# Experts in column tiles: the second half of the blocks one slot behind the first

## What is computed

```python
scores = sigmoid(h @ router_w)                     # 1152 x 16
g      = best of 4 groups of 4 experts, by the sum of its two best scores
expert = the 2 best experts in that group; w = their scores, normed to sum 1
y[t]   = sum over the 2 experts e of t:  w * ((silu(h[t] @ gate[e]) * (h[t] @ up[e])) @ down[e])
```

## Time and profile before

| | |
|---|---|
| median of three runs | 2530.28 us (2527.90 to 2533.29) |
| the profiled execution | 2531.27 us, its span 2529.4 us |
| mean granted clock of TensorE | 0.98 of full speed |
| TensorE busy | 2356.9 us, 93% of the span |
| VectorE, ScalarE, GpSimd busy | 1282.3, 816.9, 897.9 us |
| first matmul of the expert loop, last step's down | 1914.01 us, 2471.05 us |
| loaded by SyncE's queue over the whole span | 280.57 MB |

### The profile page before, as it was taken

How to read it: one execution, slowest core, us unless ns; L and a number is a source line. 1 busy time by engine, 2 the same in 40 slices (tenths; PEclk the granted TensorE clock), 3 DMA queues, 4 the chain that set the end, 5 groups by cost and what they waited for, 6 DMA issues and landing times.

```text
span 2529.4 us, 42298 instructions
## 1 busy us (share of the span) xinstructions
PE 2356.9 (93%) x16564; PEld 1602.0 (63%) x16564; DVE 1282.3 (51%) x2061; ACT 816.9 (32%) x1598; POOL 897.9 (35%) x816
## 2 busy tenths in 40 slices
PE   5999999999999999999899999999987999889994
PEld 3555787777777777776677767775463444444453
DVE  5337565666336566785959926984361101101115
ACT  3132322232222233325277732221242222222224
POOL 0001343443666556765945445661000000000003
PEclk9999999999999999999999999999998999999998
DMA  8241111112212212421201234433037556856436
GB/s 333 75 159 67 46 55 51 53 55 88 90 51 73 67 46 81 172 78 36 87 29 38 93 143 163 129 118 126 1 143 280 197 196 255 322 231 269 147 135 233
DMA packets 83401, 316.83 MB, mean 125 GB/s; under 512 B 10428, under 2 KB 37636, under 8 KB 59396
## 3 DMA queue, kind: packets, MB, share of 16 engines
q1 hardware_dynamic: 71108, 280.57, 30.4%
q0 software_dynamic: 8928, 22.03, 2.5%
q10 hardware_dynamic: 3168, 11.54, 1.1%
HBM read 711.76 MB, written 63.71 MB: 307 GB/s over the span
## 4 chain that ended last, share of the span: by engine, by line
PE 73%; DMA 9%; DVE 8%; ACT 5%; issue 3%; POOL 2%; SPq 1%; DVEq 0%; ACTq 0%; POOLq 0%
PE psum L835 24%; PE psum L723 9%; PE psum L1800 9%; PE psum L611 8%; DMA arena<-in_moe 7%; PE psum L1658 5%; PE psum L1784 4%; PE psum L1385 2%; ACT arena L2130 1%; PE psum L635 1%; PE psum L1273 1%; PE psum L1247 1%; PE psum L1769 1%; PE psum L1600 1%; PE psum L1373 1%
## 5 line engine op out<-in xcount | busy, mean ns | idle before, releaser
L835 PE MATMUL psum<-arena 128*128 128x288 f32 x3360 | 863.8, 410 | 20.1 <-POOL arena L2316 6.6
L835 PEld LDWEIGHTS psum<-arena 128*128 128x128 f32 x3360 | 623.4, 191 | 202.5 <-issue 20.2
L1800 PE MATMUL psum<-arena 128*32 128x256 f32 x5632 | 323.9, 386 | 36.5 <-DMA arena<-in_moe 35.3
L1800 PEld LDWEIGHTS psum<-arena 128*32 128x32 f32 x5632 | 178.3, 111 | 168.4 <-DMA arena<-in_moe 39.0
L723 PE MATMUL psum<-arena 128*128 128x288 f32 x896 | 217.4, 406 | 0.0
L611 PE MATMUL psum<-arena 128*128 128x384 f32 x624 | 206.0, 489 | 2.9 <-issue 2.9
L723 PEld LDWEIGHTS psum<-arena 128*128 128x128 f32 x896 | 170.2, 190 | 47.2
L2446 POOL DMA_INDIRECT y_raw<-arena,small x22 | 23.5, 1068 | 489.2 <-PE psum L1769 418.1
L2329 POOL TENSOR_TENSOR arena<-arena,cst 128x288 f32<-128x288 f32 (+1 forms) x204 | 180.2, 886 | 29.9 <-ACT arena L929 9.7
L2249 ACT ACTIVATE arena<-psum 32x512 f32<-32x512 f32 x174 | 102.4, 589 | 227.9 <-PE psum L1784 226.4
L611 PEld LDWEIGHTS psum<-arena 128*128 128x128 f32 x624 | 117.1, 190 | 88.3 <-issue 10.4
(11 more groups left out here) (601 smaller groups left out, 3407.9 us busy)
## 6 DMA issues: line engine op xcount, KB each, us to landing
arena<-in_moe SPq DMA_DIRECT2D x532, 1024.0 KB
arena<-in_gate SPq DMA_DIRECT2D x28, 1024.0 KB, 5.2
arena<-in_ada SPq DMA_DIRECT2D x12, 2048.0 KB, 9.6
gate_raw<-arena SPq DMA_DIRECT2D x128, 144.0 KB, 1.8
arena<-gate_raw SPq DMA_DIRECT2D x32, 576.0 KB, 3.9
y_rows<-arena ACTq DMA_DIRECT2D x22, 512.0 KB, 2.7
arena<-in_br SPq DMA_DIRECT2D x8, 1024.0 KB, 7.6
y_save<-arena SPq DMA_DIRECT2D x3, 2304.0 KB, 9.2
```

The lines of the kernel that those rows point to most:

```text
L835: last = nc.tensor.matmul(bank(6 + i % 2)[:, 0:NQ4], w[:, k, :], x[:, k, :], start=(k == 0), stop=(k == 3))
L1800: last = nc.tensor.matmul(bank(w)[o:o + 32, 0:256], x[:, a:a + 32], wset[i][:, 4096 * w + 512 * k + 256 * h:4096 * w + 512 * k + 256 * (h ...
```

## The change

The two sides no longer run the same product at the same time. A step is three *slots*, and side 1 runs each product one slot later than side 0:

| slot of step j | strips of side 0 | strips of side 1 |
|---|---|---|
| 0 | gate(j) | down(j-2) |
| 1 | up(j) | gate(j) |
| 2 | down(j-1) | up(j) |

The loop on TensorE goes to step 45. In a slot the calls of the two sides alternate through two generators: `rows_in` gives two matmuls of 256 columns at each turn, `rows_out` gives nothing at its first and third turn and two matmuls of 512 columns at its second and fourth. The transposes of the hidden rows of step j-1 stand between slot 0 and slot 1 of step j, `turn_block` between slot 1 and slot 2 of odd steps. There is one pair of load semaphores a slot (`e_w[s][q]`) in place of one a product, one release semaphore a slot (`e_p[s]`), and SyncE asks for the loads in the order of the slots. The first down parts are loaded inside the loop. ScalarE copies a down result out after slot 0 of step j+2 and stores a finished group at even steps; VectorE does its `dve_down` at odd steps. Cut to its core:

```diff
@@ SyncE, ahead of the loop @@
+            for at, done in ((0, e_w[0]), (4096, e_w[1])):
+                for q in range(2):
+                    a = at + 2048 * q
+                    sp.wait_ge(done[q], 16)
+                    sp.dma_start(wset[0][:, a:a + 2048], first[0][:, a:a + 2048], cond=(e0 > 0)).then_inc(done[q], 16)
+            for at, done in ((0, e_w[1]), (4096, e_w[2])):
+                for q in range(2):
+                    a = at + 2048 * q
                     sp.dma_start(wset[1][:, a:a + 2048], first[1][:, a:a + 2048]).then_inc(done[q], 16)
@@ SyncE, the loop @@
+            old, now = None, (first, (None, None))
             for j in range(NST + 1):
...
+                for q in range(2):
+                    sp.wait_ge(e_p[0], 2 * j + q + 1)
+                    if then:
+                        part_load(0, 0, q, then[0][0], e_w[0], then[1][0])
+                    if j == 0:
+                        part_load(1, 8192, q, now[0][1], e_w[0])
+                    elif j >= 2:
+                        part_load(1, 8192, q, old[0][1], e_w[0], old[1][1])
+                if then:
                     for q in range(2):
+                        sp.wait_ge(e_p[1], 2 * j + q + 1)
+                        part_load(0, 4096, q, then[0][0], e_w[1], then[1][0])
+                        part_load(1, 0, q, then[0][1], e_w[1], then[1][1])
+                if j < NST:
+                    for q in range(2):
+                        sp.wait_ge(e_p[2], 2 * j + q + 1)
+                        if then:
+                            part_load(1, 4096, q, then[0][1], e_w[2], then[1][1])
+                        part_load(0, 8192, q, now[0][0], e_w[2], now[1][0])
...
+                old, now = now, then
@@ TensorE @@
+            def rows_in(w, i, j, q):
+                x = xT[j // 2 % 2]
+                for k in range(4 * q, 4 * q + 4):
+                    for h in range(2):
+                        ... matmul of 256 columns into bank(w)[64 * i + 32 * h] ...
+                    yield last
+            def rows_out(i, j, q):
+                for k in (2 * q, 2 * q + 1):
+                    yield None
+                    for h in range(2):
+                        ... matmul of 512 columns into bank(6 + j % 2)[64 * i + 32 * h] ...
+                    yield last
+            def slot(s, j, first, second):
                 for q in range(2):
+                    pe.wait_ge(e_w[s][q], slot_loads(s, j))
+                    last = None
+                    for a, b in itertools.zip_longest(first(q), second(q)):
+                        last = b or a or last
+                    last.then_inc(e_p[s], 1)
             turn_block(0)
+            for j in range(NST + 2):
+                if j < NST:
+                    pe.wait_ge(e_xc, j // 2 + 1)
+                    if j:
+                        pe.wait_ge(e_sg, j)
+                slot(0, j, (lambda q: rows_in(0, 0, j, q)) if j < NST else none, (lambda q: rows_out(1, j - 2, q)) if j >= 2 else none)
+                if 1 <= j <= NST:
+                    pe.wait_ge(e_hid, j)
+                    ... the two transposes ...
+                if j < NST:
+                    slot(1, j, lambda q: rows_in(1, 0, j, q), lambda q: rows_in(0, 1, j, q))
                 if j % 2 and j + 1 < NST:
                     turn_block((j + 1) // 2)
+                if 1 <= j <= NST:
+                    pe.wait_ge(e_htc, j)
+                    if j >= 3:
+                        pe.wait_ge(e_ya, j - 2)
+                if j <= NST:
+                    slot(2, j, (lambda q: rows_out(0, j - 1, q)) if j else none, (lambda q: rows_in(1, 1, j, q)) if j < NST else none)
@@ ScalarE @@
             def act_down(j):
-                act.wait_ge(e_d, 2 * (j + 1))
+                act.wait_ge(e_p[0], 2 * (j + 3))
...
+            for j in range(NST + 2):
+                if j >= 2:
+                    act_down(j - 2)
+                if j < NST:
+                    act.wait_ge(e_p[1], 2 * (j + 1))
...
+                if j >= 4 and j % 2 == 0:
+                    store_block(act, (j - 4) // 2)
@@ VectorE @@
             for j in range(NST):
+                if j >= 3 and j % 2:
+                    dve_down((j - 3) // 2)
                 dve.wait_ge(e_sg, j + 1)
-                dve.wait_ge(e_u, 2 * (j + 1))
+                dve.wait_ge(e_p[2], 2 * (j + 1))
```

More of the change, by code:

```diff
@@ L1126, in _ @@
                     sp.wait_ge(o_fill, 3 * KD)
-                    for at, done in ((0, e_wg), (4096, e_wu)):
+                    for at, done in ((0, e_w[0]), (4096, e_w[1])):
                         for q in range(2):
@@ L1162, in _, with part_load @@
             sp.wait_ge(m_route, ROUTE_TAB)
-            now = None
+            def part_load(i, at, q, expert, done, changed=None):
+                a = at + 2048 * q
+                if changed is None:
+                    sp.dma_start(wset[i][:, a:a + 2048], expert[:, a:a + 2048]).then_inc(done[q], 16)
+                else:
+                    sp.dma_start(wset[i][:, a:a + 2048], expert[:, a:a + 2048], cond=(changed > 0)).then_inc(done[q], 16)
+            old, now = None, (first, (None, None))
             for j in range(NST + 1):
@@ L1185, in _ @@
                         sp.dma_start(gate_s[SLEN * b:SLEN * (b + 1)], grow[b + 1:b + 2].to_broadcast([SLEN, D])).then_inc(m_grow, 16)
-                now = then
+                old, now = now, then
             for s, c in enumerate(CHUNKS):
@@ L1771, in turn_block @@
                 last.then_inc(e_xt, 1)
-            def down_step(j):
-                pe.wait_ge(e_htc, j + 1)
-                if j >= 2:
-                    pe.wait_ge(e_ya, j - 1)
-                for q in range(2):
-                    pe.wait_ge(e_wd[q], 32 * (j + 1))
-                    for k in (2 * q, 2 * q + 1):
-                        for i in range(2):
-                            for h in range(2):
-                                o, a = 64 * i + 32 * h, P * (k % 2) + 64 * i + 32 * (k // 2)
-                                last = nc.tensor.matmul(bank(6 + j % 2)[o:o + 32], ehT[:, a:a + 32],
-                                                        wset[i][:, 8192 + 1024 * k + 512 * h:8192 + 1024 * k + 512 * (h + 1)],
-                                                        start=(k == 0), stop=(k == 3))
-                    last.then_inc(e_d, 1)
@@ new lines, in rows_out @@
+            def rows_out(i, j, q):
+                for k in (2 * q, 2 * q + 1):
+                    yield None
+                    for h in range(2):
+                        o, a = 64 * i + 32 * h, P * (k % 2) + 64 * i + 32 * (k // 2)
+                        last = nc.tensor.matmul(bank(6 + j % 2)[o:o + 32], ehT[:, a:a + 32],
+                                                wset[i][:, 8192 + 1024 * k + 512 * h:8192 + 1024 * k + 512 * (h + 1)],
+                                                start=(k == 0), stop=(k == 3))
+                    yield last
@@ new lines, in slot_loads @@
+            def slot_loads(s, j):
+                if s == 0:
+                    return 32 + sum(16 * (n + 1 < NST) + 16 * (n == 0 or 2 <= n <= NST) for n in range(j))
+                if s == 1:
+                    return 48 + 32 * j
+                return 16 + sum(16 * (n + 1 < NST) + 16 for n in range(j))
+            def slot(s, j, first, second):
+                for q in range(2):
+                    pe.wait_ge(e_w[s][q], slot_loads(s, j))
[3 more added lines that the diff above has]
+                    last.then_inc(e_p[s], 1)
@@ new lines, in none @@
+            def none(q):
+                return iter(())
+            turn_block(0)
+            for j in range(NST + 2):
[6 more added lines that the diff above has]
+                    pe.wait_ge(e_hid, j)
+                    for k in range(2):
+                        last = nc.tensor.transpose(bank(4)[:, k * P:(k + 1) * P], ehid[:, k * P:(k + 1) * P], ident)
+                    last.then_inc(e_ht, 1)
+                if j < NST:
+                    slot(1, j, lambda q: rows_in(1, 0, j, q), lambda q: rows_in(0, 1, j, q))
@@ L1804, in _ @@
                 if j % 2 and j + 1 < NST:
                     turn_block((j + 1) // 2)
-                if j:
-                    down_step(j - 1)
-                pe.wait_ge(e_hid, j + 1)
-                for k in range(2):
-                    last = nc.tensor.transpose(bank(4)[:, k * P:(k + 1) * P], ehid[:, k * P:(k + 1) * P], ident)
-                last.then_inc(e_ht, 1)
-            down_step(NST - 1)
+                if 1 <= j <= NST:
+                    pe.wait_ge(e_htc, j)
+                    if j >= 3:
+                        pe.wait_ge(e_ya, j - 2)
@@ L3118, in _ @@
                 tt(ehid, esg, bank(1)[:, 0:256], ALU.mult).then_inc(e_hid, 1)
-                if j and j % 2 == 0:
-                    dve_down(j // 2 - 1)
                 dve.wait_ge(e_ht, j + 1)
```

67 lines of the change are left out of this document (13 added, 54 removed).

## The result

The changed kernel takes 2545.8 us (median of 5 runs, 2545.5 to 2548.7) beside 2533.3 for the kernel before on the same chip: ratio **1.0056**, 95% interval 1.0041 to 1.0071. It is slower, by 0.4 to 0.7%. Its profiled execution took 2545.8 us, its span 2543.9, against 2531.3 and 2529.4 before: 14.5 us more (the medians are 12.5 apart; the profiled execution of before lies 2 us under its median here).

A forecast was written before the change was run, and what follows sets the result against it. TensorE was taken to set the pace on average, the loads only in stretches. On the profiled 2531.27 us, +7.8 + 1.5 - 3 = +6.3 gave 2537.6, less 1.0 for the median: 2536.6 us; range 2521 to 2548.

The forecast's parts named there:

- Filling and draining: Loop's two ends: 135 slots after 132 products, at most +10.4 us, less 2.6 for overlapping half-filled slots: +7.8 us.
- Mixed widths: Slots 0 and 2, 256 beside 512 columns: 0.03 us for each slot 0, +1.5 us; 19 us from above.
- widths block each other: Rival for the mixed slots: matmuls cannot overtake across strips, +76 us, 2613 us; chance 0.04.
- Part 4: Queues and chains that move, on SyncE, ScalarE, VectorE and the hidden rows: nothing added.
- The load waits: Waits at expert changes, by a ledger of 2.5 us a load: sum -3 us, bounds -15 and +10.
- Steps 23 and 24: Both sides change expert at 23: last wait shrinks by one slot, 3.5 us, and step 24's 4.7 goes; -8 us.
- the 4.7 goes: Step 24's 4.7 us above undisturbed vanishes, as down loads, two slots apart, have 5 us of DMA each.
- The three pairs 8/10, 14/15, 27/28: Side 1 changes at the first step, side 0 at the second; loads crowd neighbouring slots: +1 us a case, +3.
- The pair 19/20: Side 0's down and side 1's up fall into the same slot, four loads (10 us): +3.5 us.
- Steps 1 and 2: Loop start: a 7.09 us wait goes, but first down loads inside the loop bring 6 to 8 in step 1: -1.
- Lone changes and the store: Steps 4, 31, 34, 39 keep their slack; stores move to even steps, half a MB less in the way: -1.5 us.
- the 55.4 us lost: Loop before: 557.0 us against 501.6 undisturbed; 44.9 of waits, 0.2 of pipeline tail at each, and slow clock.

The follow-up runs named there:

- Runs 3 and 5: Changed kernel: 3, gate row's load after step 0's first half slots, 2546.8 us; 5, also one up half and all first down weights after the first gather, 2539.0 us.
- run 4: Changed kernel with the gate row late, side 1's first up weights and all first down weights asked for at the gather's indices; 2539.7 us, ratio 1.0028.
- run 7: Changed kernel with the stores of the rows issued in odd steps, as in the kernel before; 2545.8 us, ratio 1.0054.
- runs 6: Kernel before with its first down weights asked for once the first gather has landed; 2531.5 us, ratio 0.9995.

## Why the prediction was right, and where its steps were not

The forecast was slower, 2536.6 us, with a range of 2521 to 2548; it came out slower, at 2545.8. The sum of the terms was +6.3 where the profiled executions differ by 14.5. The direction was earned by the first term, filling and draining. That the time lies in the range was in part luck: the range was wide for other reasons, and it took in a term that had been left out and one with the wrong sign. Term by term:

- **Filling and draining**, +7.8 forecast, +7.0 measured (5.3 and 1.7), and 7.2 without loads. The mechanism held: three slots of 3.46 us less what neighbouring half slots overlap. The overlap is 1.7 us at the end alone (3.46 less 1.74), and 3.4 over both places (10.4 less 7.0). The 2.6 us taken for it in the sum are shown by no run; they were 0.8 short.
- **Mixed widths**, +1.5 forecast, +1.1 measured. The bound from above (19 us) and the rival "widths block each other" (76 us) are out. The Trainium skill, "TensorE: Matmul & The Clock Gate", Part 3, has it that matmuls are "strict FIFO, no reordering" in start and end. This trace does not agree for matmuls on different strips: at 2252.54 us the first down records start ahead of six gate records that stand before them in the program.
- **The first gather**: no term at all, +2.8 measured. This is the step that failed by omission. Part 4 went through SyncE's queue inside the loop and found "nothing". The diff also moves the gate row's load ahead of the gather and puts four skipped loads ahead of side 1's first ones. A transfer on another engine's queue, the gather, was the one on the path. Runs 3 and 5 show it: 1.7 us come back without the gate row's load, all 2.8 with three megabytes ahead of the gather and not four and a half. That the other 1.1 are the four skipped loads fits their place in the queue, and no run took them out alone.
- **The load waits**, -3 forecast, +3.4 measured. The ledger's sign was wrong, in these entries (differences of the extras before they are rounded):
  - Steps 23 and 24: -8 forecast, -4.2 measured. Step 23 did as forecast (-4.0), "the 4.7 goes" did not: step 24 still has 4.6 us extra, 2.3 of them a wait in slot 0 of step 25 and most of the rest the slow clock behind it. It is down weights that it waits for (without their loads the extra is gone in both kernels). Spreading the down products over two slots does not help, since their four megabytes can be asked for only when the places are free, from 2236 us on. From 2233 to 2236 us the DMA engines move 25 GB/s, nearly nothing, and from 2237 to 2250 us they move 4.07 MB for SyncE and 0.52 of a gather.
  - The three pairs 8/10, 14/15, 27/28: +3 forecast, +4.2 measured.
  - The pair 19/20: +3.5 forecast, +5.6 measured. Place and mechanism were right (side 0's down and side 1's up in one slot), the size was short.
  - Steps 1 and 2: -1 forecast, -1.2 measured. The new wait that was forecast there came. It could be had for nearly nothing in the steps themselves (run 4): with the down weights ahead of the loop these steps have 0.9 us extra.
  - Lone changes and the store: -1.5 forecast, -1.0 measured, and run 7 gives no sign that the store is the reason for any of it.

The marks given for the forecast were met in the main: undisturbed steps 0.02 to 0.03 us longer, waits for in_moe of 45.9 (38 to 46), step 20 larger. "Step 23 nearly halved" was too much: its extra fell from 12.0 to 7.9.

One reading was wrong without harm to the sum: the 55.4 us lost. The 501.6 us of 44 whole steps hold a down product in step 0, which has none, while the 557.0 end where down(43) starts. So some 59 us were lost, 55.6 of them in steps 1 to 43, and most of the rest in step 0, whose 128 records took 8.93 us and not 7.11.

The entries add up to the +3.4. What stays open: why steps 39 and 34 differ between the kernels (+1.7, -1.6), and what part of the 3.4 us is scatter; two executions of the kernel before with nearly the same loads (runs 6 and before) differ by 0.4 in the sum of steps 1 to 43, but the changed kernel has 59.0 and with its stores in odd steps 57.8, and the medians do not show the 3.4 at all (12.5 us apart with loads, 12.2 without). That filling, draining and the gather make the slowdown is shown; that the loads add to it is likely, not shown. That the two kernels' waits come so close, 55.6 and 59.0, is the outcome of gains and losses of 4 to 6 us at single coincidences.

## What to carry to other kernels

Staggering two streams by a slot costs the fill and the drain for sure, some 7 us here, and moves load waits from some coincidences to others; list the coincidences that the new order makes (same slot, one step apart, two steps apart) before counting on those that it breaks. When a diff reorders one engine's DMA queue, look at the first transfer of every other queue that falls into the same stretch. And look at what stands ahead of an urgent load in its issuing queue: asking for eight small loads three steps later took 5 us off one step, while no variant of the large change came below the kernel before.

## What the hardware showed

- Matmuls with 32-column weights on different strips pass each other: 512 and 256 columns start side by side every 0.43 us, two records overtake six that stand before them (2252.54 us), and two half-filled products of 3.5 us pass in 5.38 us together.
- After 2.27 us without work a half slot ran at a granted clock of 0.52 and took 3.5 us, where 1.73 is usual.
- A gather of GpSimd beside SyncE's 1 MB loads moved as many packets as they did (184 beside 186), in smaller packets, a third of the DMA engines' time. Its tokens were turned 11.1 us after the routing product, where 6.3 is the time with the engines free.
- A load of SyncE whose condition is false still holds the queue: with its wait, 0.35 us each (four in 1896.36 to 1897.74 us).
